# Attention probabilities turned by VectorE and device memory instead of TensorE, in a two-layer hybrid decoder trunk

## What is computed

```python
def _causal_attention(q, k, v):
...
        s = jnp.einsum('bqhd,bkhd->bhqk', qi, k, preferred_element_type=jnp.float32) * scale
...
        s = jnp.where(kpos[None, :] <= qpos[:, None], s, -jnp.inf)
        p = jax.nn.softmax(s, axis=-1)
        return jnp.einsum('bhqk,bkhd->bqhd', p.astype(v.dtype), v)
...
def reference(x, positions, ln_g, w_in, w_out, ...):
    for l in range(DEPTH):
        h = _rmsnorm(x, ln_g[l])
        u = h @ w_in[l]
...
        y_a = _gla(...) * jax.nn.silu(g_a)
        y_b = _ssd_mixer(...)
        y_c = _mla(...) * jax.nn.silu(g_c)
...
        y_d = _dilated_attention(dq, dk, d_v.reshape(Bsz, S, DIL_H, DIL_HD)) * jax.nn.silu(g_d)
        y = jnp.concatenate([y_a, y_b, y_c, y_d], axis=-1).astype(x.dtype)
        x = x + y @ w_out[l]
    return x
```

## Time and profile before

| | |
|---|---|
| median of 3 runs | 813.11 us (812.63 to 813.15) |
| the profiled execution, its own time | 812.43 us |
| its span, first to last instruction | 810.6 us, 10807 instructions |
| TensorE busy | 804.6 us, 99% |
| VectorE busy | 611.7 us, 75% |
| ScalarE busy | 470.8 us, 58% |
| GpSimd busy | 95.0 us, 12% |
| DMA moved | 165.63 MB, mean 204 GB/s |

### The profile page before, as it was taken

How to read it: one execution, slowest core, us unless ns; L and a number is a source line. 1 busy time by engine, 2 the same in 40 slices (tenths; PEclk the granted TensorE clock), 3 DMA queues, 4 the chain that set the end, 5 groups by cost and what they waited for, 6 DMA issues and landing times.

```text
span 810.6 us, 10807 instructions
## 1 busy us (share of the span) xinstructions
PE 804.6 (99%) x3972; PEld 682.2 (84%) x3972; DVE 611.7 (75%) x1076; ACT 470.8 (58%) x764; POOL 95.0 (12%) x134
## 2 busy tenths in 40 slices
PE   8999999999999999999999999999999999999998
PEld 5888887999888888888888888889998888888886
DVE  6678899887897766678965977989779977665452
ACT  6666544867955667443556465447687575664431
POOL 7100000120413211000000000002105042100000
PEclk9999999999999999999999999999999999999999
DMA  8956535576686947655676655365766688566563
GB/s 332 356 206 209 185 130 165 163 248 190 199 242 204 288 158 234 205 186 181 187 251 182 201 156 185 112 193 166 239 194 213 203 243 269 189 203 208 187 190 118
DMA packets 50004, 165.63 MB, mean 204 GB/s; under 512 B 6368, under 2 KB 7056, under 8 KB 49952
## 3 DMA queue, kind: packets, MB, share of 16 engines
q1 hardware_dynamic: 44736, 149.98, 56.9%
q0 software_dynamic: 4896, 14.75, 6.5%
q10 hardware_dynamic: 320, 0.21, 0.1%
HBM read 155.47 MB, written 9.45 MB: 203 GB/s over the span
## 4 chain that ended last, share of the span: by engine, by line
PE 90%; DVE 7%; issue 2%; DMA 1%; SPq 0%; ACT 0%; DVEq 0%
PE gemm L735 27%; PE gemm L744 27%; PE gemm L736 26%; DVE arena L1377 3%; DVE w_lo L1416 2%; PE pairs L915 1%; PE pairs L890 1%; PE pairs L885 1%; PE pairs L886 1%; PE pairs L856 1%; PE pairs L801 1%; DVE arena L1505 1%; PE pairs L898 1%; PE pairs L929 1%; DMA u<-in_xT_dram 1%
## 5 line engine op out<-in xcount | busy, mean ns | idle before, releaser
L1416 DVE TENSOR_TENSOR w_lo<-raw,w_hi 128x1024 fp32r<-128x1024 f32 (+2 forms) x279 | 322.6, 1167 | 144.5 <-ACT w_hi L1050 143.6
L735 PE MATMUL gemm<-w_hi,a_hi 128*128 128x512 f32 (+2 forms) x1080 | 415.6, 385 | 0.0
L736 PE MATMUL gemm<-w_hi,a_lo 128*128 128x512 f32 (+2 forms) x1080 | 409.0, 379 | 0.0
L1050 ACT ACTIVATE w_hi<-raw 128x1024 fp32r<-128x1024 f32 (+2 forms) x279 | 278.4, 1012 | 198.9 <-PE gemm L744 134.3
L744 PE MATMUL gemm<-w_lo,a_hi 128*128 128x512 f32 (+2 forms) x1080 | 278.2, 379 | 0.3
L735 PEld LDWEIGHTS gemm<-w_hi,a_hi 128*128 128x128 f32 x1080 | 202.9, 188 | 35.9 <-issue 1.7
L736 PEld LDWEIGHTS gemm<-w_hi,a_lo 128*128 128x128 f32 x1080 | 203.0, 188 | 33.2
L744 PEld LDWEIGHTS gemm<-w_lo,a_hi 128*128 128x128 f32 x1080 | 199.5, 188 | 36.4 <-DVE w_lo L1416 1.9
L632 POOL TENSOR_TENSOR st<-st,powers 128x4 f32<-128x4 f32 (+2 forms) x8 | 4.1, 513 | 367.6 <-ACT arena L1131 213.2
L1252 ACT ACTIVATE arena<-arena,st 128x128 f32<-128x128 f32 (+1 forms) x32 | 13.1, 444 | 30.3 <-DVE st L1711 30.3
L1083 ACT ACTIVATE u<-gemm,st 128x512 f32<-128x512 f32 (+2 forms) x36 | 21.3, 644 | 15.8 <-PE gemm L744 15.8
(11 more groups left out here) (211 smaller groups left out, 665.3 us busy)
## 6 DMA issues: line engine op xcount, KB each, us to landing
raw<-in_weights_dram SPq DMA_DIRECT2D x225, 512.0 KB, 4.3
raw<-in_weights_dram SPq DMA_DIRECT2D x38, 384.0 KB, 3.7
raw<-in_weights_dram SPq DMA_DIRECT2D x16, 344.0 KB, 3.3
y_squares<-arena POOLq DMA_DIRECT2D x6, 512.0 KB, 4.9
arena<-y_squares POOLq DMA_DIRECT2D x24, 128.0 KB, 4.8
x<-in_x_dram SPq DMA_DIRECT2D x4, 512.0 KB, 6.1
o<-ssd_rows SPq DMA_DIRECT2D x8, 256.0 KB, 5.5
param_rows<-in_params_dram SPq DMA_DIRECT2D x2, 904.0 KB, 8.0
```

Source lines behind the costliest of these rows:

```text
L735: pe.matmul(acc_t[t], a_hi[:, k, tok[t]], hi, start=k == 0, stop=False)
L736: pe.matmul(acc_t[t], a_lo[:, k, tok[t]], hi, start=False, stop=False)
L1050: A_(w_hi[:, g % SPLIT, 0:c], raw[:, g % RAW, 0:c], ACT.Copy).then_inc(hi_done, 1)
L1416: TT(w_lo[:, g % SPLIT, 0:c], raw[:, g % RAW, 0:c], w_hi[:, g % SPLIT, 0:c].bitcast(F32), ALU.subtract).then_inc(split_done, 1)
```

## The change

TensorE's four `PT` jobs a layer are taken out. In their place VectorE turns `Pb` in 32x32 squares (`probs_squares`, two instructions for 2 x 384 elements a partition) into the region of `u` that `dil q` and `dil k` held, GpSimd sends it out (384 KB) and fetches it back in four DMAs into the same place, and ScalarE's copy into `PT` now reads it there, with the squares put in order, waits for `squares_in`, and stands at slot `O` + 1 instead of `PT` + 3. The values jobs go from slots 94, 98, 104, 108 to 96, 101, 107, 111; `dil S 0` and `dil S 1` from 99 and 103 to 98 and 102. `dil k squares` go from slot 93 to 92, and the `mla P` squares stand at slots 93 and 97; the `dil P` squares follow `taps` at slots 101 and 105. GpSimd's order of sends and fetches is rewritten.

```diff
@@ -207,9 +207,8 @@
     PE_AT[f"gla level {_n}"] = 26 + 2 * _n
 PE_AT |= {"gla out": 45, "ssd cum": 50, "ssd gcol": 54, "ssd CB": 56,
           "mla cT": 64, "mla q 0": Q_AT, "mla q 1": Q_AT, "mla kv 0": KV_AT,
-          "mla kv 1": KV_AT, "ssd Y": 76, "mla qT": 85, "mla kT": 86, "mla rT": 87, "mla S 0": 89, "mla PT 0": 92,
-          "mla S 1": 93, "mla O 0": 94, "mla PT 1": 96, "mla O 1": 98, "dil S 0": 99,
-          "dil PT 0": 102, "dil S 1": 103, "dil O 0": 104, "dil PT 1": 106, "dil O 1": 108,
+          "mla kv 1": KV_AT, "ssd Y": 76, "mla qT": 85, "mla kT": 86, "mla rT": 87, "mla S 0": 89,
+          "mla S 1": 93, "mla O 0": 96, "dil S 0": 98, "mla O 1": 101, "dil S 1": 102, "dil O 0": 107, "dil O 1": 111,
           "yT 3": 114}
...
@@ -396,7 +394,10 @@
             SQUARES[f"y {_j}"] = A(_j * 1024, 1024), A(_j * 1024, 1024), _n
         SQUARES["ssd y"] = A(4096, 1024), A(4096, 1024), 81
         SQUARES["dil q"] = A(5632, 1024), A(5632, 1024), 92
-        SQUARES["dil k"] = A(6656, 1024), A(6656, 1024), 93
+        SQUARES["dil k"] = A(6656, 1024), A(6656, 1024), 92
+
+        for _i in range(2):
+            SQUARES[f"mla P {_i}"] = SQUARES[f"dil P {_i}"] = (u[:, _i, COL["dq"]:COL["dq"] + 768],) * 2 + ((93, 97)[_i],)
 
         def by_f(row):
             return row.rearrange("p (k f b) -> p f k b", f=4, b=32)
@@ -466,7 +467,7 @@
         first_in, first_hi, first_lo, last_tile = sem("first_in"), sem("first_hi"), sem("first_lo"), sem("last_tile")
         warm = sem("warm")
         squares_out_done, squares_in = ({name: sem(name.replace(" ", "_") + end) for name in SQUARES} for end in ("_squares_out", "_squares_in"))
-        squares_d = {name: nc.dram_tensor(name.replace(" ", "_") + "_squares", (P, 4 * S), F32, kind="Internal").ap() for name in SQUARES}
+        squares_d = {name: nc.dram_tensor(name.replace(" ", "_") + "_squares", SQUARES[name][0].shape, F32, kind="Internal").ap() for name in SQUARES}
         setup_chain = sem("setup_chain")
         x_updated = sem("x_updated")
         row_out, row_in = sem("row_out"), [sem(f"row_in_{i}") for i in range(SSD_H // 2)]
@@ -649,11 +650,20 @@
                 squares_out(l, "ssd y")
                 squares_back(l, "ssd y")
                 squares_out(l, "dil q")
+                squares_out(l, "dil k")
+                squares_out(l, "mla P 0")
                 rsqrt("ssd rs", brs, bss)
-                squares_out(l, "dil k")
+                squares_back(l, "mla P 0")
                 squares_back(l, "dil q")
                 squares_back(l, "dil k")
-                for name in ("y 1", "y 0", "y 2"):
+                for name in ("mla P 1", "y 1"):
+                    squares_out(l, name)
+                    squares_back(l, name)
+                squares_out(l, "y 0")
+                squares_out(l, "dil P 0")
+                squares_back(l, "dil P 0")
+                squares_back(l, "y 0")
+                for name in ("dil P 1", "y 2"):
                     squares_out(l, name)
                     squares_back(l, name)
 
@@ -920,15 +930,6 @@
                                 last = pe.matmul(ps[:, r, c0:c1], mrT[rows, 0, i, qs], mrT[rows, 1, i, 0:c1 - c0], start=False, stop=c0 == P)
                     last.then_inc(*signal("pe", f"{m} S {i}"))
 
-                def probs_T(m, i):
-
-                    pe.wait_ge(*(act if m == "mla" else dve)(f"{m} P {i}"))
-                    ps = bank()
-                    for r in range(2):
-                        for c in range(3):
-                            last = pe.transpose(ps[:, r, c * P:(c + 1) * P], Pb[:, r, c * P:(c + 1) * P], ident)
-                    last.then_inc(*signal("pe", f"{m} PT {i}"))
-
                 def values(m, i, v):
 
 
@@ -972,10 +973,6 @@
                             scores("mla", i, (mqT, mkT), True)
                         elif name.startswith("dil S"):
                             scores("dil", i, (dqT, dkT), False)
-                        elif name.startswith("mla PT"):
-                            probs_T("mla", i)
-                        elif name.startswith("dil PT"):
-                            probs_T("dil", i)
                         elif name.startswith("mla O"):
                             values("mla", i, mv)
                         elif name.startswith("dil O"):
@@ -1254,8 +1251,11 @@
                     last.then_inc(*signal("act", f"{m} P {i}"))
 
                 def probs_T(m, i):
-                    act_.wait_ge(*pe(f"{m} PT {i}"))
-                    A_(PT[:, :, :], pair_of(f"{m} PT {i}")[:, :, 0:384], ACT.Copy).then_inc(*signal("act", f"{m} PT {i}"))
+                    act_.wait_ge(squares_in[f"{m} P {i}"], 16 * 4 * (l + 1))
+                    if (m, i) != ("mla", 0):
+                        act_.wait_ge(*pe(f"{m} O 0" if i else "mla O 1"))
+                    to, squares = PT.rearrange("p r (c i a) -> p i (r c) a", i=4, a=32), SQUARES[f"{m} P {i}"][1].rearrange("p (i x a) -> p i x a", i=4, a=32)
+                    A_(to, squares, ACT.Copy).then_inc(*signal("act", f"{m} PT {i}"))
 
                 for place, n in enumerate(STREAM):
                     hi(place, n)
@@ -1341,7 +1341,7 @@
                             for i in range(2):
                                 if n == slot(f"{m} S {i}"):
                                     probs(m, i)
-                                if n == slot(f"{m} PT {i}"):
+                                if n == slot(f"{m} O {i}", 1):
                                     probs_T(m, i)
                         if n == 94:
                             ssd_sq()
@@ -1695,8 +1695,8 @@
                     v.wait_ge(*pe(f"{m} S {i}"))
                     if (m, i) == ("mla", 0):
                         v.wait_ge(*me(f"gated {GB}"))
-                    if i:
-                        v.wait_ge(*pe(f"{m} PT {i - 1}"))
+                    if (m, i) != ("mla", 0):
+                        v.wait_ge(*me(f"{m} P 0 squares" if i else "mla P 1 squares"))
                     ps = pair_of(f"{m} S {i}")
                     mk = cmask if m == "mla" else dadd
 
@@ -1719,6 +1719,16 @@
                             last = v.tensor_tensor_reduce(out=Pb[:, r, c0:c1], in0=Pb[:, r, c0:c1], in1=dmul[:, 2 * P - (c1 - c0):], scale=1.0,
                                                           scalar=0.0, op0=ALU.mult, op1=ALU.add, accum_out=sm[i][:, j:j + 1])
                     last.then_inc(*sig(f"dil P {i}"))
+
+                def probs_squares(m, i):
+
+                    v.wait_ge(*(act if m == "mla" else me)(f"{m} P {i}"))
+                    if (m, i) == ("mla", 0):
+                        v.wait_ge(*me("dil k squares"))
+                    to = SQUARES[f"{m} P {i}"][0].rearrange("p (f r c a) -> p r f c a", f=4, r=2, c=3)
+                    for r in range(2):
+                        last = v.transpose(to[:, r], Pb[:, r].rearrange("p (c f b) -> p f c b", c=3, f=4))
+                    last.then_inc(*sig(f"{m} P {i} squares"))
 
                 def out_heads(m, i):
 
@@ -1846,6 +1856,7 @@
                                     smax(m, i)
                                     if m == "dil":
                                         taps(i)
+                                        probs_squares(m, i)
                                 if n == slot(f"{m} O {i}"):
                                     out_heads(m, i)
                         if l + 1 < DEPTH and n in X_NEXT:
@@ -1862,6 +1873,9 @@
                             ssd_norm()
                         if n == 99:
                             gated(GA)
+                        for i in range(2):
+                            if n == SQUARES[f"mla P {i}"][2]:
+                                probs_squares("mla", i)
                         for j in Y_TURN:
                             if n == Y_TURN[j] and j != GC:
                                 y_squares(j)
```

More of the change, by code:

```diff
@@ L223 @@
     for _i in range(2):
-        LAST_READER |= {f"{_m} S {_i}": ("dve", f"{_m} max {_i}"), f"{_m} PT {_i}": ("act", f"{_m} PT {_i}"),
-                        f"{_m} O {_i}": ("dve", f"{_m} O {_i}")}
+        LAST_READER |= {f"{_m} S {_i}": ("dve", f"{_m} max {_i}"), f"{_m} O {_i}": ("dve", f"{_m} O {_i}")}
 LAST_READER |= {f"yT {_j}": ("dve", f"yT {_j}") for _j in range(4)}
@@ L249 @@
         "mla cT, ssd Y, mla qT, mla kT, mla rT, "
-        "mla S 0, mla PT 0, mla S 1, mla O 0, mla PT 1, mla O 1, dil S 0, dil PT 0, dil S 1, dil O 0, "
-        "dil PT 1, dil O 1, yT 3",
+        "mla S 0, mla S 1, mla O 0, dil S 0, mla O 1, dil S 1, dil O 0, dil O 1, yT 3",
     "act":
@@ L257 @@
         "mla kv 0, mla kv 1, mla rs 1 sum, dil rs 0 sum, evac 8, dil rs 1 sum, mla qT, mla kT, evac 9, "
-        "mla rT, mla P 0, ssd rs sum, mla PT 0, mla P 1, evac 10, mla PT 1, dil q, dil P 0, dil PT 0, "
-        "evac 11, dil P 1, dil PT 1, yT 0, yT 1, yT 2, evac 12, yT 3",
+        "mla rT, mla P 0, ssd rs sum, mla P 1, mla PT 0, evac 10, dil q, dil P 0, mla PT 1, "
```

(2 more changed lines are left out.)

## The result

The changed kernel takes **818.08 us** (median of 7 runs, 816.15 to 822.06) against 812.91 for the kernel before in the same session (812.53 to 813.15): +5.2 us between the medians. The ratio of the means is 1.0075, with a 95% interval from 1.0061 to 1.0089. The forecast was 809.2, with 813.2 as the upper end. It was wrong in sign. The profiled execution is the fastest of the seven: 816.15, with a span of 814.3, 3.7 more than before. What follows accounts for this run; the median lies 1.9 us above it, and no trace shows where that went.

What follows compares the result with a forecast made beforehand. The prediction took TensorE, busy for 99% of the span, to bound the kernel. It summed -5.4 + 1.5 + 0 = -3.9 us, giving 808.5 for the profiled execution and 809.2 for the median, range 807.4 to 813.2.

Steps and rivals of the forecast that it cites:

- What leaves TensorE: Four transpose jobs in each of two layers leave TensorE's path at 0.67 us each: 5.4 us gained.
- The first trip: Layer 0, `mla P 0` squares out by DMA and back: sent at 254.6, landing at 266.6 us.
- The deadline: Before `mla O 1`, TensorE waits for ScalarE's second `PT` copy: 1.5 us in layer 0, none in layer 1.
- Transfers were quicker there: Layer 1: 4.4 us out and 4.0 for the last piece, landing at 264.9 in layer 0's clock, no wait.
- The other trips: Later transfers, `dil P 0`, `dil P 1` and `dil k` back: all land before they are needed, adding 0 us.
- second copy: ScalarE's copy into `PT` for `mla O 1`: ready 18.6 us after the first landing, asked for at 283.7.
- (c): Rival, ScalarE at slot 97 behind `mla P 0`'s landing: waits of 5.05 and 4.15 us, 816.9 us, chance 0.14.
- what would show the forecast wrong: A landing past 268, or TensorE waiting before `dil O` or for weights.
- Range and chances: Whole kernel: 807.4 to 813.2 us; faster 0.71, same 0.15, slower 0.14; the forecast itself 0.47.

## Why the prediction was wrong

- **What leaves TensorE: right, a little high.** 5.4 us forecast, 4.8 by the span without trips. The remaining 0.6 wasn't located.
- **The first trip: right.** Landing at 266.4 for 266.6, with the first fetch at 260.1 for 260.0: the 5.2 us taken between 3.1 and 6.8 were about right for this transfer. The 3.3 us that the `ssd rs` pair should hold GpSimd were 1.4 (254.91 to 256.33), which changed nothing, since GpSimd then waited for the landing.
- **The deadline: right in place, size half right.** The wait before `mla O 1` was 1.0 us in layer 0 (1.5) and 1.2 in layer 1 (0). "Transfers were quicker there" failed: from send to first fetch this trip took 5.8 us in both layers (254.34 to 260.12, 654.05 to 659.85). A row of the kernel before, with four transfers fewer, is no price for layer 1. The sum was 2.2 for 1.5.
- **"The other trips": the step that failed.** It followed `dil P 0`, `dil P 1` and `dil k`, found them covered (they were), and stopped. `y 2` was never costed, though it is next on GpSimd's queue and the change puts its send behind the landing of `dil P 1`. The sum has a 0 where that wait belongs; 6.2 us were measured there (0.6 and 5.55). The paragraph had the numbers. Its second copy is ready at T = 266.6 + 18.6 = 285.2, so `dil P 1`'s fetches end at T + 11.1 + 0.35 + 5.2 + 0.2 + 2.2 = 304.3 (the trace: 304.6), 0.8 later than `y 2` was sent before. With 5.2 out and 4.9 for the last piece, `y 2` would land at 304.3 + 5.2 + 0.2 + 1.65 + 4.9 = 316.3; with 6.8 and 6.9, at 319.9. TensorE's need, worked back by the chain of 8.45 us from where it came to `yT 3` (0.92 us after the start of the last L754), was 317.3 in layer 0 and 717.0 in layer 1. (The first could be forecast: 326.21 for the last L744 before, less four jobs of 0.67, plus the 1.5 of wait, is 325.0, and it came at 324.85.) So there was 1 us of cover in the centre and none at the upper end, where the kernel before had over 4: landed near 314 (the last fetch issued at 308.5, 5.7 us to landing), needed at 327.13 - 8.45 = 318.7. That should have been a rival of at least the weight of (c). ScalarE went on behind the landings at 317.87 and 720.87. The trace of the kernel before even had the nearer row. Its `y 0`, as large as `y 2`, was sent right behind the four fetches of `y 1` (GpSimd, layer 0):

```profile
276.42 0.56 POOL L617 DMA_DIRECT2D y_squares<-arena  x1
283.79 2.18 POOL L624 DMA_DIRECT2D arena<-y_squares  x4 [6.81 <-DMA y_squares<-arena]
```

That is 7.4 us to the first fetch, where the forecast's centre is 5.4 with the 0.2 to wake. With 7.4 the landing comes to 304.3 + 7.4 + 1.65 + 4.9 = 318.2, past TensorE's need in the centre.
- **The chain behind it.** The prediction worked ScalarE's queue behind slot 97 with care and didn't ask the same at slot 114, where the same pattern stands: a landing, then an evacuation with two table loads, then the hi that VectorE needs. TensorE also comes there 1.9 us earlier than before (724.52 for 726.38), since what it gained earlier is spent at the next fixed landing.
- **Rival (c)** named the sign and almost the size (816.9), at the wrong place: slot 97 of both layers instead of slot 114. That its number lies near is luck. The sentence on what would show the forecast wrong, TensorE waiting before `dil O` or for weights, didn't name `yT 3` either.
- **Range and chances.** Most of the chance was spread over the size of one transfer. The order behind another transfer of the same kind decided.

## What to carry to other kernels

When a step is added to a queue, follow every later item of that queue to its reader, not only the added ones, and work back from TensorE's need at each of them with the same range of transfer times. In a hand-written order, a wait for a DMA should stand behind everything on its engine that others need sooner: moved two slots, the same late transfer cost nothing. Expect a gain in TensorE's time to shorten the slack of every fixed landing behind it by as much.
